# Two-block transformer layer on one core: the order of matmuls inside each step of the first block's attention

## The reference

```python
# NSA attention: 8 heads in 2 groups, two of the branches (selected, window) over all earlier keys
s_s = einsum('bghqd,bgqkd->bghqk', qb, ks) * scale - slope * d_s
p_s = masked_softmax(s_s, ...);  o_s = einsum('bghqk,bgqkd->bghqd', p_s, vs)
...
return gb[..., 0:1] * o_c + gb[..., 1:2] * o_s + gb[..., 2:3] * o_w
# MLA attention: 8 heads, keys of 64 + 32 columns
s = (einsum('bhqd,bhkd->bhqk', qn, k_nope) + einsum('bhqd,bkd->bhqk', qr, k_rope)) * scale
p = masked_softmax(s, kpos <= qpos);  einsum('bhqk,bhkd->bhqd', p, v)
...
y = sigmoid(g_a) * (o_a @ w_branch_a) + sigmoid(g_b) * (o_b @ w_branch_b)
```

## Time and profile before

| | us |
|---|---|
| median of 3 runs (3366.64 to 3369.36) | 3367.29 |
| the profiled execution, its own time | 3366.43 |
| span of its trace | 3364.7 |
| PE busy in the span | 3323.5 |

### The profile page before, as it was taken

The page is one execution under the profiler, slowest core; times in us unless marked ns, Lnnn a source line. Parts: engine busy times, 40 slices in busy tenths (PEclk is TensorE's granted clock), DMA queues, the critical chain, the costliest instruction groups (busy, mean ns, idle before and its releaser), DMA issues.

```text
span 3364.7 us, 40394 instructions
## 1 busy us (share of the span) xinstructions
PE 3323.5 (99%) x16582; PEld 2697.2 (80%) x16582; DVE 1743.3 (52%) x2955; ACT 1197.8 (36%) x2020; POOL 258.8 (8%) x219
## 2 busy tenths in 40 slices
PE   9999999999999999999999999999999999999999
PEld 7888887778888888887877888888778777878887
DVE  7666446665565733333656643334463555464433
ACT  3222336643222332223456332224332344233322
POOL 0000210002000200011200100004012000020000
PEclk9999999999999999999999999999999999999999
DMA  7565322123565533323211322322222223133332
GB/s 260 203 214 186 128 83 75 41 81 117 188 231 190 198 100 94 100 88 117 93 45 32 107 88 85 109 86 96 88 72 72 66 85 118 57 101 94 95 107 80
DMA packets 120359, 376.33 MB, mean 112 GB/s; under 512 B 13296, under 2 KB 28272, under 8 KB 120176
## 3 DMA queue, kind: packets, MB, share of 16 engines
q1 hardware_dynamic: 120176, 373.76, 34.1%
HBM read 371.61 MB, written 2.10 MB: 111 GB/s over the span
## 4 chain that ended last, share of the span: by engine, by line
PE 94%; DVE 3%; ACT 2%; issue 0%; POOL 0%; DMA 0%; SPq 0%; DVEq 0%; ACTq 0%; POOLq 0%
PE ps L469 27%; PE ps L471 26%; PE ps L470 26%; PE ps L720 2%; PE ps L612 2%; PE ps L742 2%; PE ps L507 1%; PE ps L509 1%; PE ps L508 1%; DVE s_wl L1588 1%; ACT s_wh L1045 0%; PE ps L582 0%; PE ps L583 0%; PE ps L584 0%; PE ps L535 0%
## 5 line engine op out<-in xcount | busy, mean ns | idle before, releaser
L1588 DVE TENSOR_TENSOR s_wl<-s_raw,s_wh 128x1024 fp32r<-128x1024 f32 (+3 forms) x645 | 708.5, 1100 | 825.1 <-ACT s_wh L1045 824.4
L469 PE MATMUL ps<-s_uh,s_wl 128*128 128x512 f32 x2760 | 1096.3, 397 | 7.1 <-DVE s_ul L1645 3.8
L471 PE MATMUL ps<-s_ul,s_wh 128*128 128x512 f32 x2760 | 1076.2, 390 | 0.0
L470 PE MATMUL ps<-s_uh,s_wh 128*128 128x512 f32 x2760 | 1075.3, 390 | 0.0
L1045 ACT ACTIVATE s_wh<-s_raw 128x1024 fp32r<-128x1024 f32 (+3 forms) x645 | 587.7, 913 | 646.2 <-PE ps L471 469.3
L469 PEld LDWEIGHTS ps<-s_uh,s_wl 128*128 128x128 f32 x2760 | 518.6, 188 | 123.7 <-issue 15.7
L471 PEld LDWEIGHTS ps<-s_ul,s_wh 128*128 128x128 f32 x2760 | 518.4, 188 | 109.7
L470 PEld LDWEIGHTS ps<-s_uh,s_wh 128*128 128x128 f32 x2760 | 518.9, 188 | 105.4 <-issue 2.2
L469 PE MATMUL ps<-s_fh,s_wl 128*128 128x512 f32 x960 | 373.4, 389 | 0.0
L470 PE MATMUL ps<-s_fh,s_wh 128*128 128x512 f32 x960 | 373.4, 389 | 0.0
L471 PE MATMUL ps<-s_fl,s_wh 128*128 128x512 f32 x960 | 373.4, 389 | 0.0
(11 more groups left out here) (439 smaller groups left out, 3355.9 us busy)
## 6 DMA issues: line engine op xcount, KB each, us to landing
s_raw<-w SPq DMA_DIRECT2D x616, 512.0 KB, 3.6
s_raw<-w SPq DMA_DIRECT2D x96, 192.0 KB, 2.4
s_raw<-w SPq DMA_DIRECT2D x64, 256.0 KB, 2.7
s_raw<-w SPq DMA_DIRECT2D x19, 128.0 KB, 2.0
s_x<-x SPq DMA_DIRECT2D x4, 512.0 KB, 5.4
out<-s_x SPq DMA_DIRECT2D x8, 256.0 KB, 2.2
s_raw<-w SPq DMA_DIRECT2D x4, 420.0 KB, 3.9
s_crow<-crow SPq DMA_DIRECT2D x2, 512.0 KB, 5.4
```

The costliest lines, as they stand in the source:

```text
L469: TE.matmul(o, w_lo(i, k), h, start=first, stop=False)
L470: TE.matmul(o, w_hi(i, k), h, start=False, stop=False)
L471: return TE.matmul(o, w_hi(i, k), l, start=False, stop=last)
L1588: V.tensor_tensor(wl[w][:, 0:n], raw[t % NRAW][:, 0:n], wh[w][:, 0:n].bitcast(F32), SUB).then_inc(*s_lo.up(("lo", t)))
```

## The change

`gate_slots` gives one list of pieces per step, with the same pieces in the same step as before. In a step PE now does: values of r-2, turns of r-1 half 0, scores of r, turns of r-1 half 1, and then all gate pieces in one run. ACT takes both copies of half 0 and half 1 before the four exponentials, where it alternated copies and exponentials by half. DVE, POOL and SP keep their order.

```diff
 def gate_slots():
-    counts = [(0, 0, 0)] * 2 + [(0, 1, 1)] * 6 + [(0, 2, 2), (0, 2, 2), (0, 1, 1), (0, 1, 1)] * 4 + [(2, 1, 0), (0, 0, 1)]
+    counts = [0] * 2 + [2] * 6 + [4, 4, 2, 2] * 4 + [3, 1]
     out, n = [], 0
-    for slots in counts:
-        out.append([])
-        for c in slots:
-            out[-1].append([(k // 4, k % 4) for k in range(n, n + c)])
-            n += c
+    for c in counts:
+        out.append([(k // 4, k % 4) for k in range(n, n + c)])
+        n += c
...
                     if r - 2 == len(rounds) - 1:
                         s_pe.mark(("attend", st))
+                if 1 <= r <= len(rounds):
+                    round_turns(r - 1, 0)
                 if r < len(rounds):
                     round_scores(r)
-                before_turns, between, after_turns = slots[r]
-                for n in before_turns:
-                    piece(*n)
-                if 1 <= r <= len(rounds):
-                    round_turns(r - 1, 0)
-                for n in between:
-                    piece(*n)
                 if 1 <= r <= len(rounds):
                     round_turns(r - 1, 1)
-                for n in after_turns:
+                for n in slots[r]:
                     piece(*n)
...
-                for half in range(2):
-                    if 1 <= r <= len(rounds):
-                        round_turned(r - 1, half)
-                    if r < len(rounds):
-                        round_exps(r, half)
-                for n, quarter in sum(slots[r], []):
+                if 1 <= r <= len(rounds):
+                    round_turned(r - 1, 0)
+                    round_turned(r - 1, 1)
+                if r < len(rounds):
+                    round_exps(r, 0)
+                    round_exps(r, 1)
+                for n, quarter in slots[r]:
```

More of the change, by code:

```diff
@@ L1264, in mix @@
                 if r >= 1:
-                    for n, quarter in sum(slots[r - 1], []):
+                    for n, quarter in slots[r - 1]:
                         if quarter == 3:
                             gate(n)
-                for half in range(2):
-                    if 1 <= r <= len(rounds):
-                        round_turned(r - 1, half)
-                    if r < len(rounds):
-                        round_exps(r, half)
-                for n, quarter in sum(slots[r], []):
+                if 1 <= r <= len(rounds):
[5 more added lines that the diff above has]
+                for n, quarter in slots[r]:
                     if quarter == 0:
```

## The result

| | before | after |
|---|---|---|
| median, us | 3367.97 (11 runs, 3365.97 to 3369.36) | 3375.93 (11 runs, 3372.92 to 3378.67) |
| ratio to before | | 1.0023 [1.0014, 1.0032] |
| span of the profiled execution | 3364.7 | 3375.1 |
| PE busy in it | 3323.5 | 3328.4 |

The change costs 8.0 us, by the interval 4.7 to 10.8. That is inside the range, 1.7 above the predicted time, and slower by just over 0.2%.

The account below looks back on a forecast made before the run. PE's queue was taken as the bound, busy 3323.5 of 3364.7 us (99%). Terms -0.3 + 3.2 - 0.6 + 0.1 + 0.9 + 3.6 = +6.9 us gave 3374.2 us, range 3369 to 3380.5.

Parts of the forecast that it names:

- Alternation of fp32r and fp32: Gate runs between transposes: removing one run in 46 steps gives 0.01 us each, taken as -0.3 us.
- Changes of tiling, NSA: NSA steps: reordered array tiling changes cost 0.60 us a step against 0.50, +3.2 us over 32 steps.
- Changes of tiling, MLA: MLA steps: tiling changes cost 0.15 us a step against 0.20, -0.6 us over 12 steps.
- Banks in the body: Loop body: half 1's transposes need half 0's PSUM bank copied out; +0.1 us, upper end +5.
- late p: Loop body, step 11: p comes later in the new order but in time, by 0.3 to 0.6 us at worst.
- no wait is left to win: Body of both loops: PE busy for all of 39.00 us from 531 to 570, so no waits remain there.
- the body waits: Rival: body steps wait for copies or p coming 0.3 us late, +5 to +10 us on top; chance 0.15.
- The end: Step 24: no scores between the halves, so half 1 waits 0.45 us for a copy per layer, +0.9 us.
- The start: First steps of each loop: transposes wait for softmax, +1.3 us first layer, +2.3 second, together +3.6.
- Hidden: Rival: the values-to-transposes change is hidden, 44 x 0.15 goes, about +0.3 us in all; chance 0.17.
- faster: Rival: 46 gate-run entries give back 4.1 us, with hidden transposes and a cheaper start, sum -5 us; chance 0.08.

Follow-up runs that it names:

- gates between: Kernel before with, in steps 3 to 23, all gate pieces in one run between the two halves of turns, scores ahead, ACT's order old; 3375.71 us, ratio 1.0023.
- scores first: Kernel before with PE doing values, scores, both halves of turns, then all gates in one run, ACT copying both halves first; 3387.64 us, ratio 1.0058.
- old start and end: Kernel before with the changed order on PE and ACT in steps 3 to 23 only, steps 0 to 2 and last two as before; 3370.87 us, ratio 1.0007.
- the control: Kernel before with the same instructions in the same order on every engine, only the loop written another way; 3367.88 us, ratio 1.0000.

## Why the prediction was right

The total, +6.9 forecast, is 7.4 in the loops and 8.0 by the medians. By its own steps:

- **Alternation of fp32r and fp32, -0.3.** With "gates between" the NSA steps at i = 0 are 0.04 shorter than before and those at i = 3 equal. Those at i = 1 are 0.04 longer, with a wait in them. So it is 0.00 to 0.04 each, and the step's reading of early and late starts (0.08 against 0.09) was right: in step 11 the gate runs gave back 0.08 and the transposes lost their early start.
- **Changes of tiling, NSA, 32 x 0.10 = +3.2.** Right in kind; 0.125 was measured over 15 steps of each layer, so 32 steps cost 4.0. The term was 0.8 too small. Values to transposes is 0.21, and the six transposes between values and scores are slow by 0.05, as foreseen. What I had too low is the way from transposes into 64-row scores: I took 0.15, and it is 0.20, as from values. That makes 0.15 a step, which three of the four kinds show to 0.02, and the fourth has its 0.12 of old waits to give back. The rule of the Trainium skill, "TensorEngine Tiling (Array Packing)", Key Properties, that a change of tiling mode drains the TensorE, fits: each added change costs time here. That the time is a drain, no row can show. The estimate of 0.05 us that I had worked out from the Trainium skill, "TensorE: Matmul & The Clock Gate", Step-by-step: what each phase is for, is less than half of the 0.125 that the runs show.
- **Changes of tiling, MLA, 12 x -0.05 = -0.6.** 0.06 to 0.07 in each of ten steps. The other two lie in the start.
- **Banks in the body, +0.1, and late p.** No idle row between 535 and 704 us. From start to start the steps at i = 1 hold 0.06 of waiting for half 1's bank, eight times, 0.5 us in all, where I had called it even; against that they lost the 0.12 for the gate piece. The latter I had not seen: "no wait is left to win" was read from the busy time alone. The rival "the body waits" fell, though the margins it feared are real: "scores first" pays 0.43 a step where they are gone.
- **The end, 0.45 in each layer.** 0.46 measured, released by ACT at the third turned tile, as written. It needs no change of ACT's order.
- **The start, +1.3 and +2.3.** 1.43 and 1.73 measured, 3.2 for 3.6. The first wait was put at 1.3 and is 1.13; the second at 1.9 + 0.1 and is 1.78 and 1.51. The second layer was mis-sized: I let POOL's slopes slow DVE's scaling of round 1 there as before (1.53 for two tiles in the earlier trace rows), but p is made later now, when POOL is all but through, and they take 0.86 (rows in the last section). Half of that is chance: POOL's last slopes also begin earlier here, 1680.59 - 1674.57 = 6.0 us into the loop, where it was 1675.44 - 1667.92 = 7.5 in the earlier trace rows. The split between the layers is also loose, since the unchanged start takes 13.93 or 13.3 in different executions. Against 13.32 ("old start and end") the first layer's start costs 2.0, so that +1.3 was met there is in part luck: the profile before had the longer of its starts.
- **The rivals.** "Hidden" and "faster" needed values-to-transposes to be free. It is not, by the 0.21 from 598.42 to 598.63 and the 0.05 in the transposes behind it.

Some 0.6 us between 7.4 and 8.0 isn't accounted for, and lies within the interval.

## What to carry to other kernels

When PE is busy all the time, moving its work costs what the new neighbours cost: list the runs by the part of the array they use (128 rows, 64 rows, 64 columns) and count the changes per step, before and after. Here each added one cost 0.125 and 0.16 us a step, while a change between fp32r and plain fp32 at the same tiling cost at most 0.04. And compare from start to start: a wait of 0.12 us in each fourth step stood in a profile without idle time. Then look at the first and the last steps of the loop apart from the body: work that only fills time in the body (a piece, the next scores) is what covers a softmax or a copy there, and moving it out cost 4.1 of the 7.4 us. An order used in the body alone would have had less than half of the loss, and in the MLA steps alone none.

## What the runs showed of the hardware

The same start of the loop, with the same order, takes 13.93 us in one execution and 13.32 in another, and it takes 13.93 and 13.34 in the two layers of the kernel before. PE's second wait there is 1.20 in the earlier trace rows and 0.60 in the earlier trace rows. It goes with what POOL's slopes meet on DVE. They begin 519.73 - 516.93 = 2.8 us into the loop in the first layer, 1672.30 - 1667.92 = 4.4 in the second. In the first layer DVE's scaling of round 0's half 1 (two 128x256) takes 1.47, in the second 0.62, and what comes behind it is late. Timeline of POOL before, then of DVE:

```profile
519.73 3.07 POOL L2308 TENSOR_SCALAR s_slope<-s_dist 128x512 f32<-128x512 f32 x2 [34.63 <-DMA s_dist<-dist]
...
1672.30 3.07 POOL L2308 TENSOR_SCALAR s_slope<-s_dist 128x512 f32<-128x512 f32 x2 [36.18 <-DVE s_mfew L1850]
```

```profile
520.60 1.47 DVE L1866 TENSOR_SCALAR s_mP<-s_mP,s_mfew 128x256 f32<-128x256 f32 x2
...
1671.16 0.62 DVE L1866 TENSOR_SCALAR s_mP<-s_mP,s_mfew 128x256 f32<-128x256 f32 x2
```

When the slopes begin doesn't tell the two cases apart by much. In the second layer of the control they begin 1673.47 - 1670.61 = 2.86 into the loop, the scaling takes 0.64 and the start 13.33 (timeline of POOL):

```profile
1673.47 3.06 POOL L2310 TENSOR_SCALAR s_slope<-s_dist 128x512 f32<-128x512 f32 x2 [34.66 <-PE ps L728]
```

Beside POOL, DVE's scaling of two 128x384 tiles takes 1.53. In the changed kernel (timeline of DVE, then of POOL) it takes 0.75 in the first layer, 0.3 us after POOL's last slopes, and 0.86 in the second, where it overlaps their last 0.3 us:

```profile
529.21 0.75 DVE L1860 TENSOR_SCALAR s_mP<-s_mP,s_mfew 128x384 f32<-128x384 f32 x2
...
1683.32 0.86 DVE L1860 TENSOR_SCALAR s_mP<-s_mP,s_mfew 128x384 f32<-128x384 f32 x2
```

```profile
525.89 3.06 POOL L2302 TENSOR_SCALAR s_tmp<-s_dist 128x512 f32<-128x512 f32 x2
...
1680.59 3.06 POOL L2302 TENSOR_SCALAR s_tmp<-s_dist 128x512 f32<-128x512 f32 x2
```

The Trainium skill, "GPSIMD Engine Reference", Key points, says that POOL shares its SBUF interfaces with VectorE and contends with some of its instructions. The trace agrees for this one, with up to a factor of two. Not each one beside POOL is slow: the same pair in the first layer before, at 524.62, takes 0.97 in all, though POOL's slopes run to 526.07.
